# First stage of a two-block transformer kernel: output projection, norm, residual and router with tokens on partitions

## The chip, the cores and the metric

One core of one Trainium2 chip runs the whole program. The metric is device time in microseconds (us). The kernel before took 1844.75, 1839.3 and 1840.13 us in three timed runs; the median is 1840.13.

TensorE (PE) multiplies: a product takes 128-row weights (the stationary operand) and streams columns of the moving operand into PSUM, where up to 512 float32 columns of 128 partitions fill one bank. VectorE (DVE) and ScalarE (ACT) work on rows along the partitions, GpSimd (POOL) is a further engine, and SyncE (SP) issues most of the loads. Everything is float32; a float32 product appears in the trace as two instructions.

## The reference, cut to what matters

The model has a first block (attention with low-rank latents, a Fourier mixer, a mixture of 32 experts) and a second block of two layers. The input is 256 tokens of 1024 features. The change is between the attention of the first block and its experts:

```python
mix_x = jnp.concatenate([att_x, four_x], axis=-1) @ w_out[l]
x = x + g1 * rms_norm(mix_x, norm_attn_post[l])
hx2 = modulate(x, norm_ffn_pre[l], sh2, sc2)        # rms_norm(x, g) * (1 + sc2) + sh2
logits = h @ w_router + b_router                     # h = hx2
top_logit, top_idx = lax.top_k(logits, 4)
gates = jax.nn.softmax(top_logit, axis=-1)
# tokens of each expert in a block of their own, then per block:
g = jnp.minimum(xb @ w_gate[e] + b_gate[e], 7.0)
u = jnp.clip(xb @ w_up[e] + b_up[e], -7.0, 7.0)
y = (g * jax.nn.sigmoid(1.702 * g) * (u + 1)) @ w_down[e] + b_down[e]
```

The vectors g1, sh2, sc2 and g2 are four of the six rows of `silu(c) @ w_mod + b_mod`.

## The kernel before, in words

The program is a list of instructions for each engine, in a fixed order, with semaphores between them. An engine runs its own list in order, so that a wait holds everything behind it on that engine. The stages are `stage_first` (up to the router's tables), `stage_experts`, and `stage_second` for the second block.

**What lies on the partitions.** In `stage_first` features lie on partitions: `xT` and `mixT` are `[128, 8, 256]`, feature block times token. x is turned into `xT` at the very start (`turned(x, 4)`, L437, copies at L797 and L991). The output projection (`outward`, L649 to L658) makes 8 output blocks of 128 features by 8 input blocks: 64 products of 256 columns, in four PSUM banks (`BANKS`). The norm over features is then a sum over partitions: ScalarE squares each bank's copy (L943), a product with ones adds over partitions (L703), a 128x256 root and reciprocal follow (L947, L1162), the gain per feature is a scale per partition (L936), and VectorE multiplies and adds into `xT` (L1167, L1170). For the second norm the squares are collected by VectorE (L1159). The logits are four partial sums on 4 x 32 partitions (L713), added by a product with `quad` (L735), and h2 is `g2x` turned back into PSUM (L720), scaled per token and shifted (L1205).

**Routing.** VectorE takes the top eight of the logits (L1185), their indices (L1188), builds the 0/1 `mask` of the four picks (L1197, L1200), and the gates. TensorE counts, for each token and expert, the tokens ahead of it, by the strict triangle `stri` (L742), and the tokens of each expert (L745). VectorE makes `key` of it (rank of a picked token, -1 otherwise, L1229 and L1232), and the number of 64-token blocks of each expert, `more`, by four dependent comparisons (L1222 to L1225). TensorE turns key and gate (L756, L757), adds up `more` to the first block of each expert (L749 to L751), and spreads key and gates over 48 possible passes by `pick` (L768 to L770). The engines read the integer `table` for the loops.

**The experts.** `stage_experts` runs one pass for each block of 64 tokens (33 here: 32 experts and one with two blocks). A pass gathers the tokens by a product with the 0/1 matrix `sel` (L1370), turns them (L1376), adds biases (L1383), multiplies by gate and up weights (L1402) and down weights (L1455), and combines. The weights of one expert are 12.6 MB, in six parts. `ring` has ten places of 2 MB; `load_ahead` (L217) fills all ten from `stage_first`, each as soon as what it holds is no longer used. In the stage SyncE issues a part when a place is freed (L1334), which first happens after the first half of the gate products of pass 0.

**The order around the change.** SyncE's list has: w_mod blocks (2 MB each, L386, into three places in turn), w_out, one expert part after the last modulation sum, the expert biases, three and one parts after attention (`pv_ps`), one after `sh_ps`, three after the last projection product (`mix_ps` 4), and the last, where mix and h2's operands lay, after h2 (`h2_ok` 2). VectorE sums w_mod with `modulate_all` (L1025), in pieces between its attention steps. `keep_busy` (L133) issues filling products of 256 columns on TensorE.

Of the kernel before, what the change touches and what calls it, by code (L numbers as in the profile page):

```python
# [37 lines left out]
PAD = 16  # L38

# [23 lines left out]
for _name, _n in (("ident", P), ("ones", P), ("tri", QT * SEQ), ("iota", P), ("causal", QT * SEQ), ("cmpvalid", QT), ("etri", EXPERTS), ("gate16", 16), ("pad", 6),  # L63
                  ("twin", HD), ("heads16", 8), ("swap", P), ("ccos", P), ("csin", P), ("stri", QT * SEQ),
                  ("cos", SEQ), ("sin", SEQ), ("ncos", QT * SEQ), ("nsin", QT * SEQ), ("quad", EXPERTS), ("pad_last", 32)):
    CONST[_name] = (_at, _n)
    _at += _n
# [4 lines left out]
def shape_constants():  # L72
# [24 lines left out]
    strict = (n[:, None] < n[None, :]).astype(np.float32).reshape(QT, P, SEQ).transpose(1, 0, 2)  # L97
    put("tri", incl)
    put("stri", strict)
# [28 lines left out]
    put("quad", (np.arange(P)[:, None] % EXPERTS == e[None, :]).astype(np.float32))  # L128
# [91 lines left out]
def stage_first(nc, m, t):  # L220
# [6 lines left out]
    m.table = m.moe.sb("table", [1, PASSES + 1 + 2 * EXPERTS], I32)  # L227
# [12 lines left out]
    wr = s.sb("wr", [P, C, EXPERTS])  # L240
    br = s.sb("br", [1, EXPERTS])
# [8 lines left out]
    def early_tile(*shape):  # L250
# [4 lines left out]
        if len(shape) == 2:  # L255
# [28 lines left out]
    cosr, sinr, rb_q, rb_m = (m.spare[:, SEQ * j:SEQ * (j + 1)] for j in range(4))  # L284
# [10 lines left out]
    mixT, g2x = hT, hT  # L295
    mrow = zone[:, D:2 * D].rearrange("p (b n) -> p b n", b=2)
    acc1 = zone[:, 2 * D - 512:2 * D]
    idle = stats[:, 20:21]
    MOD_SLOT = (0, 4, 8, 0, 4, 8, 16, 8)
# [12 lines left out]
    rows_t, cols_ready, ssum, stds, rstds, normed, x_ps, copied_a, copied_v, silu_ready, silu_zero, mods_ps, mods_sb, moda_ps = (  # L312
        m.sem(n) for n in ("rows_t", "cols_ready", "ssum", "stds", "rstds", "normed", "x_ps", "copied_a", "copied_v", "silu_ready",
# [9 lines left out]
    msum_ps, msum_sb, modc_ps, modc_raw, modc_ok, crow_ps, sh_ps, sh_ok, mix_ps, mix_sb, mix_sq, mix_g, x1_mul, x1_ok, g2x_ok, x1_sq, x1_acc, lg_ps, part_ok, h2_ps, h2_ok = (  # L323
        m.sem(n) for n in ("msum_ps", "msum_sb", "modc_ps", "modc_raw", "modc_ok", "crow_ps", "sh_ps", "sh_ok", "mix_ps", "mix_sb", "mix_sq", "mix_g", "x1_mul",
                           "x1_ok", "g2x_ok", "x1_sq", "x1_acc", "lg_ps", "part_ok", "h2_ps", "h2_ok"))
# [3 lines left out]
    def scratch(shape, parts=P):  # L329
# [7 lines left out]
        if len(shape) == 2:  # L337
# [3 lines left out]
    part = scratch((SEQ,))  # L341
# [6 lines left out]
    key = scratch((QT, EXPERTS))  # L348
# [3 lines left out]
    tmp = scratch((3, PASSES), EXPERTS)  # L352
# [3 lines left out]
    logit_sb, top8, top_i, top_f, picked, peak, exped, g_chain, rank_ps, key_ok, more_chain, more_ps, table_ok, turned_ps, turned_sb, spread_ps, spread_sb = (  # L356
        m.sem(n) for n in ("logit_sb", "top8", "top_i", "top_f", "picked", "peak", "exped", "g_chain", "rank_ps", "key_ok", "more_chain",
                           "more_ps", "table_ok", "turned_ps", "turned_sb", "spread_ps", "spread_sb"))

    with nc.Block() as block:  # L360

        @block.gpsimd
        def _(pool):
# [4 lines left out]
            pool.memset(acc, 0.0).then_inc(zeroed, 1)  # L368

        @block.sync  # L370
        def _(sp):
# [49 lines left out]
            sp.wait_ge(sh_ps, 2)  # L421
            load_ahead(sp, m, t, 0, (3,))
# [7 lines left out]
        def _(pe):  # L430
# [10 lines left out]
            pe.wait_ge(x_in, 16)  # L441
            turned(x, 4)
# [23 lines left out]
            pe.wait_ge(copied_a, 2)  # L466
            pe.wait_ge(copied_v, 2)
# [183 lines left out]
            def outward(ks, cs, first=False, last=False):  # L651

                for k in ks:
# [2412 lines left out]
```

## Time and profile before

| what | us |
|---|---|
| timed runs | 1844.75, 1839.3, 1840.13 |
| median | 1840.13 |
| profiled execution | 1844.5 |
| its span | 1842.6 |
| TensorE busy | 1798.7 (98%) |
| VectorE busy | 601.2 (33%) |
| ScalarE busy | 372.7 (20%) |
| GpSimd busy | 10.9 (1%) |
| HBM read | 552.43 MB, 303 GB/s over the span |

Times in the rows are counted from the start of the span. A row of the timeline is a run of like instructions: start, length of the run, engine, line, operation, operands, and in brackets how long the engine had been idle and what ended that. Engine utilisation is no measure of need here: filling products count as busy.

### The profile page before, as it was taken

To read this page: it belongs to the slowest core of one execution; us is meant where nothing else is said; L and a number is where in the kernel's file an instruction comes from. 1 tells how busy PE (TensorE), PEld (TensorE's weight loads), DVE (VectorE), ACT (ScalarE), POOL (GpSimd) and SP (SyncE) were. 2 spreads that over 40 slices of the span, in tenths; PEclk is the share of its full clock that TensorE was granted. 3 is DMA by queue.
4 is the path that set the end of the run, shared out by engine and by line. 5 is a ranking of instruction groups with operands and counts; after the bars stand their busy time and mean duration, and the time that the engine had idled before them with its cause. 6 is when DMAs were issued, how large, how long until landed. Compare 5 with 4: busy or idle time off the path is not lost. (4 is left out here: it accounts for less than half of the span.)

```text
span 1842.6 us, 23153 instructions
## 1 busy us (share of the span) xinstructions
PE 1798.7 (98%) x9221; PEld 979.9 (53%) x9222; DVE 601.2 (33%) x1260; ACT 372.7 (20%) x725; POOL 10.9 (1%) x14
## 2 busy tenths in 40 slices
PE   7999999999999999999999999999999999999998
PEld 6757533333333333333333335767995466699843
DVE  1854410111111011111111113544655544345555
ACT  3221411111111111111111113332220033222101
POOL 0000000000000000000000000000000000000001
PEclk9999899999999999999999999999999999999999
DMA  9996599999999999999999999532446543124452
GB/s 370 393 188 270 237 412 430 431 430 431 433 431 432 430 431 432 431 431 431 432 432 431 431 430 358 174 140 92 151 149 241 160 183 137 46 92 147 151 175 99
DMA packets 104495, 558.61 MB, mean 303 GB/s; under 512 B 17128, under 2 KB 33997, under 8 KB 78701
## 3 DMA queue, kind: packets, MB, share of 16 engines
q1 hardware_dynamic: 101876, 553.06, 74.4%
q10 hardware_dynamic: 2554, 4.63, 1.8%
q8 instruction: 47, 0.77, 0.2%
q14 instruction: 18, 0.15, 0.0%
HBM read 552.43 MB, written 5.23 MB: 303 GB/s over the span
## 5 line engine op out<-in xcount | busy, mean ns | idle before, releaser
L1402 PE MATMUL ps<-ring,xs 128*64 128x512 f32 x2112 | 467.0, 593 | 10.9 <-DMA ring<-in_w_up 5.5
L1402 PEld LDWEIGHTS ps<-ring,xs 128*64 128x64 f32 x2112 | 150.7, 137 | 315.8 <-issue 291.6
L1455 PE MATMUL ps<-ring,actT 128*64 128x512 f32 x1056 | 233.9, 595 | 0.0
L2279 PE MATMUL ps<-ring 128*128 128x512 f32 x448 | 192.8, 592 | 0.0
L1528 DVE TENSOR_SCALAR hT<-ps 128x512 f32<-128x512 f32 x33 | 22.8, 692 | 449.7 <-PE ps L1402 449.7
L1455 PEld LDWEIGHTS ps<-ring,actT 128*64 128x64 f32 x1056 | 72.9, 137 | 158.7 <-issue 136.8
L2279 PEld LDWEIGHTS ps<-ring 128*128 128x128 f32 x448 | 84.9, 190 | 105.7 <-issue 105.7
L2014 PE MATMUL ps<-hT,ring 128*128 128x256 f32 x512 | 117.9, 383 | 3.5 <-ACT hT L1653 2.1
L1530 DVE TENSOR_SCALAR hT<-ps 128x512 f32<-128x512 f32 x33 | 22.8, 692 | 267.3 <-PE ps L1402 267.3
L2014 PEld LDWEIGHTS ps<-hT,ring 128*128 128x128 f32 x512 | 94.7, 190 | 22.2 <-issue 5.4
L2233 PE MATMUL ps<-hT,ring 128*128 128x128 f32 x768 | 93.4, 275 | 0.2 <-ACT hT L1653 0.2
L2233 PEld LDWEIGHTS ps<-hT,ring 128*128 128x128 f32 x768 | 89.5, 192 | 0.4 <-ACT hT L1653 0.3
L1506 ACT COPY y<-ps 128x512 f32<-128x512 f32 x33 | 19.3, 586 | 246.5 <-PE ps L1455 246.5
L1413 PE MATMUL ps<-y,selT 64*128 64x512 f32 x272 | 67.6, 615 | 0.7 <-ACT y L1506 0.7
L1499 ACT COPY xs<-ps 128x512 f32<-128x512 f32 x33 | 19.4, 587 | 236.2 <-PE ps L1376 236.2
L1370 PE MATMUL ps<-x_sb,sel 128*64 128x512 f32 x272 | 65.9, 606 | 0.3 <-PEq L360 0.3
L2233 PE MATMUL ps<-sq,ring 128*128 128x128 f32 x512 | 62.1, 275 | 0.0
L2233 PE MATMUL ps<-spare,ring 128*128 128x128 f32 x512 | 62.1, 275 | 0.0
L1495 ACT ACTIVATE hT<-hT 128x512 f32<-128x512 f32 x33 | 20.8, 630 | 193.7 <-DVE hT L1528 193.7
L2233 PEld LDWEIGHTS ps<-sq,ring 128*128 128x128 f32 x512 | 59.6, 192 | 0.0
L2233 PEld LDWEIGHTS ps<-spare,ring 128*128 128x128 f32 x512 | 59.6, 192 | 0.0
L2197 PE MATMUL ps<-x_sb,ring 128*128 128x256 f32 x256 | 57.4, 381 | 0.9 <-ACT x_sb L1636 0.9
(457 smaller groups left out, 1792.0 us busy)
## 6 DMA issues: line engine op xcount, KB each, us to landing
ring<-in_w_gate SPq DMA_DIRECT2D x64, 2048.0 KB, 29.0
ring<-in_w_down SPq DMA_DIRECT2D x64, 2048.0 KB, 29.1
ring<-in_w_up SPq DMA_DIRECT2D x64, 2048.0 KB, 27.3
ring<-in_mlp_w SPq DMA_DIRECT2D x16, 2048.0 KB, 8.7
ring<-in_mlp_w SPq DMA_DIRECT2D x32, 1024.0 KB, 5.4
ring<-in_w_mod SPq DMA_DIRECT2D x8, 2048.0 KB, 11.8
ring<-in_odd_w_in SPq DMA_DIRECT2D x6, 2048.0 KB, 10.1
ring<-in_w_mod SPq DMA_DIRECT2D x16, 512.0 KB, 11.0
```

What stands on the lines that cost most here:

```text
L1370: mm = pe.matmul(ps[SLOTS * half:SLOTS * (half + 1), TURN, :], sel[:, i, :], h2[:, i, half * 512:(half + 1) * 512], start=(i == 0), stop=( ...
L1402: mm = pe.matmul(ps[SLOTS * half:SLOTS * (half + 1), bank, :], xs[:, c % 4, c // 4 * SLOTS:(c // 4 + 1) * SLOTS], weights(v, 8 * part + c) ...
L1413: mm = pe.matmul(ps[:, COMB + 2 * i + half, :], selT[rows, i, :], y[rows, :], start=False, stop=stop, skip_group_check=True)
L1455: mm = pe.matmul(ps[SLOTS * half:SLOTS * (half + 1), Y, :], actT[:, f % 4, f // 4 * SLOTS:(f // 4 + 1) * SLOTS], weights(v, 16 + f)[:, hal ...
L1495: act.activation(sig, g, ACT.Sigmoid, scale=ALPHA).then_inc(sig_ok, 1)
L1499: act.copy(xs[:].rearrange("p b n -> p (b n)"), ps[:, TURN, :]).then_inc(xs_sb, 1)
L1528: v.tensor_scalar(g, ps[:, G, :], LIMIT, None, ALU.min).then_inc(g_ok, 1)
L1530: v.tensor_scalar(u, ps[:, U, :], -LIMIT, LIMIT, ALU.max, ALU.min).then_inc(u_ok, 1)
L2014: mm = pe.matmul(ps[:, bank, 0:SEQ], w[:, c, at:at + P], hT[:, c, :], start=(c == 0), stop=(c == C - 1))
L2197: mm = pe.matmul(ps[:, turn.banks[k], (d % 2) * SEQ:(d % 2 + 1) * SEQ], w[c // 4][:, c % 4, d * P:(d + 1) * P], mixT[:, c, :], start=(firs ...
L2233: mm = pe.matmul(out[:, i, :], weight[:, k, i * P:(i + 1) * P], token[:, k, :], start=(opens and k == 0 and i == 0), stop=(k == 3), skip_g ...
L2279: return pe.matmul(product_bank(layer, n), token, weight, start=(c == 0), stop=(c == PAIRS - 1))
```

## The change

It does the following, all in float32.

1. The output projection puts tokens on partitions: for token half `i` and feature half, 8 products of 512 columns each, 32 in all. Token half 0 is finished first, and its norm, residual, turning and logits are put between the products of half 1.
2. g1, 1 + sc2 (times their norm gains) and sh2 are spread to all partitions as rows by one-partition products (`rows_of`), and lie in `grow`, `scrow` and `shrow`. The gains come by four loads of a 512-row repeated on 32 partitions, which SyncE issues ahead of w_mod block 5, behind a wait for the rotary part.
3. The sums of squares are ScalarE's `accum_out` along the row; the root and reciprocal are 128x1. The residual is one fused multiply and add per 512 columns on x, which is loaded a second time. x is not turned at the start; `xT` is made from x1 afterwards.
4. The router's weights are multiplied by the scale column once (`wrm`), and the logits are 8 products per half from `xT`. h2 is a multiplication on GpSimd and a fused multiply and add on VectorE.
5. The rank is a product `mask.T @ rank`, experts on partitions, where `rank` is the strict triangle with 512 (`MARK`) on the diagonal. A picked token has its rank plus 512; `base` takes 512 off, so that others are negative. The number of blocks is one comparison with 4 limits and a sum.
6. The biases of pass 0 are put at the end of `stage_first`, and TensorE's `passes` load ahead of `turn_x`.
7. One expert part (`0, 3`) is issued after `msum_ps` instead of `sh_ps`.

```diff
-    put("stri", strict)
+    ranking = (n[:, None] < n[None, :]).astype(np.float32) + MARK * np.eye(SEQ)
+    put("rank", ranking.reshape(QT, P, SEQ).transpose(1, 0, 2))
...
+                if c == 5:
+                    sp.wait_ge(rope_done, 4)
+                    for j, name in enumerate(("norm_attn_post", "norm_attn_post", "norm_ffn_pre", "norm_ffn_pre")):
+                        src = t[name]
+                        sp.dma_start(gainrow[32 * j:32 * (j + 1), :], bass.AP(src.tensor, 512 * (j % 2), [[0, 32], [1, 512]])).then_inc(
+                            gainrow_in, 16)
                 second_part(c)
...
+            sp.wait_ge(pt_ps, HEADS)
+            sp.dma_start(x[:], stack(t["x"][0])).then_inc(x_in, 16)
+            sp.wait_ge(msum_ps, 1)
+            load_ahead(sp, m, t, 0, (3,))
             sp.wait_ge(pv_ps, HEADS)
...
-            pe.wait_ge(x_in, 16)
-            turned(x, 4)
+            keep_busy(m, pe, 4, 7)
...
                 for k in ks:
+                    i, half = k // 2, k % 2
                     for c in cs:
-                        for d in (2 * k, 2 * k + 1):
-                            mm = pe.matmul(ps[:, BANKS[k], (d % 2) * SEQ:(d % 2 + 1) * SEQ], w_out[:, c, d * P:(d + 1) * P], mixT[:, c, :],
+                        mm = pe.matmul(ps[:, BANKS[k], :], mixT[:, c, i * P:(i + 1) * P], w_out[:, c, 512 * half:512 * (half + 1)],
...
+            pe.wait_ge(pv_sb, 6)
+            rows_of(0, 0, 4)
+            outward((0, 1), (4, 5), last=True)
             pe.wait_ge(modc_raw, 2)
+            rows_of(0, 2, 2)
+            pe.wait_ge(row_a, 1)
+            pe.wait_ge(row_v, 1)
+            rows_of(1, 0, 4)
+            outward((2,), (6, 7, 0, 1), first=True)
...
+            outward((2,), (2, 3, 4, 5), last=True)
+            turned_back(0)
+            outward((3,), (6, 7, 0, 1), first=True)
+            logits(0, {0: 1, 4: 2})
+            outward((3,), (2, 3, 4, 5), last=True)
+
+            keep_busy(m, pe, 7, 4)
+            turned_back(1)
+            logits(1, {0: 3, 4: 4, 6: 5})
+            rank = cst(m, "rank")
+            pe.wait_ge(picked, 4)
+            pe.matmul(ps[0:EXPERTS, 5, 0:1], mask[:, 0, :], ones[:, 0:1], start=True, stop=False)
+            pe.matmul(ps[0:EXPERTS, 4, 0:SEQ], mask[:, 0, :], rank[:, 0:SEQ], start=True, stop=False)
+            keep_busy(m, pe, 7, 2)
+            pe.wait_ge(picked, 8)
...
+            row(1, 4, grow)
+            mix_power(0)
+            row(2, 2, scrow)
+            row(3, 4, shrow)
             act.wait_ge(crow_ps, 1)
+            act.copy(crow[:], ps[:, 3, 0:EXPERTS]).then_inc(crow_ok, 1)
+            x1_power(0)
+            mix_power(1)
+            x1_power(1)
...
+            row(1, 5, grow)
+            v.wait_ge(row_a, 1)
+            v.wait_ge(row_v, 1)
+            gained(0)
+            row(2, 3, scrow)
+            row(3, 5, shrow)
+            v.wait_ge(x_in, 32)
+            residual(0)
+            back(0, 0, 0, 4)
+            back(0, 1, 0, 4)
+            variance(0)
+            deviation(0)
+            v.wait_ge(row_a, 3)
+            v.wait_ge(row_v, 3)
+            scaled(0)
+            v.wait_ge(crow_ok, 1)
+            route(0)
+            gained(1)
+            residual(1)
+            back(1, 0, 0, 4)
+            variance(1)
+            back(1, 1, 0, 2)
+            back(1, 1, 2, 2)
+            deviation(1)
+            route(1)
...
+            for i in range(QT):
+                for half in range(2):
+                    k, cols = 2 * i + half, slice(512 * half, 512 * (half + 1))
+                    pool.wait_ge(x1_ok, k + 1)
+                    pool.tensor_tensor(mix[:, k, :], x[:, i, cols], scrow[:, cols], ALU.mult).then_inc(h2_mul, 1)
...
             gather()
-            biases(((0, G), (1, U)))
+            n = passes(pe)
+            pe.wait_ge(bdown_in, 32)
             pe.wait_ge(xrow_sb, 1)
             turn_x()
             keep_busy(m, pe, Y, 1)
-            n = passes(pe)
-            pe.wait_ge(bdown_in, 32)
```

The list with `mix_power` is ScalarE's, the one with `gained` VectorE's, the loop of `pool` GpSimd's. The helpers: `mix_power(i)` squares the two banks of half i and takes the root, `x1_power(i)` the same for x1; `gained` multiplies PSUM by `grow`; `residual` is x + mix * r; `turned_back(i)` and `back` make `xT` of half i; `route(i)` runs from the logits' fused multiply and add to the mask of half i; `scaled(i)` finishes h2 of half i, the last one after the tables.

## Rows read from the trace of the kernel before

**Rows 1.** Windows: stretch, length, busy PE PEld DVE ACT POOL, PEclk, DMA share, GB/s.
```profile
200.00:201.00 1.00, 0.77 (x6) 0.36 (x7) 0.27 (x1) 0.80 (x3) 0.00 (x0) 1.00 1.03 442
203.00:204.00 1.00, 1.00 (x5) 0.91 (x6) 0.46 (x3) 0.98 (x2) 0.00 (x0) 0.50 0.99 426
226.00:230.00 4.00, 4.00 (x20) 1.45 (x22) 0.00 (x0) 2.00 (x3) 0.00 (x0) 1.00 0.01 2
400.00:1120.00 720.00, 710.34 (x3412) 250.11 (x3408) 100.68 (x237) 121.00 (x183) 0.00 (x0) 1.00 1.01 431
```

**Rows 2.** Waits of TensorE, 225 to 1130 us: total, times, longest.
```profile
PE ps L1402 <- DMA ring<-in_w_up: 5.5, 6, 1.0
```

**Rows 3.** Timeline of TensorE: start, length, line, operands, number of instructions.
```profile
165.12 10.53 PE L656 MATMUL ps<-hT,ring 128*128 128x256 f32 x48
180.66 1.87 PE L694 MATMUL ps<-wr,modc 128*128 128x32 f32 x16
...
186.34 2.94 PE L703 MATMUL ps<-ring,consts_sb 128*128 128x256 f32 x12
...
218.61 3.68 PE L1370 MATMUL ps<-x_sb,sel 128*64 128x512 f32 x8 [0.30 <-PEq L360]
222.22 1.29 PE L1383 MATMUL ps<-brows,now 32*64 32x512 f32 x8
...
225.91 7.09 PE L1402 MATMUL ps<-ring,xs 128*64 128x512 f32 x32 [1.28 <-issue]
```

**Rows 4.** Timeline of SyncE: the issues of expert parts.
```profile
186.54 0.33 SPq L217 DMA_DIRECT2D ring<-in_w_gate  x1
...
208.75 0.33 SPq L217 DMA_DIRECT2D ring<-in_w_down  x1
229.60 3.76 SPq L1334 DMA_DIRECT2D ring<-in_w_down  x2
```

**Rows 5.** Timeline of VectorE: picks, h2, gate steps, last copy.
```profile
205.28 1.06 DVE L1200 SCALAR_TENSOR_TENSOR zone<-consts_sb,zone 128x32 f32<-128x32 f32 x6
206.26 2.47 DVE L1205 SCALAR_TENSOR_TENSOR x_sb<-ps,stats,ring 128x1024 f32<-128x1024 f32 x2
208.64 0.21 DVE L1209 TENSOR_TENSOR zone<-zone 128x64 f32<-128x64 f32 x1
208.89 0.22 DVE L1211 TENSOR_REDUCE zone<-zone 128x2 f32<-128x64 f32 x1
...
217.47 0.25 DVE L1255 COPY gates<-ps 128x96 f32<-128x96 f32 x1
```

**Rows 6.** Timeline of ScalarE: a Square, and a sum read out.
```profile
184.74 0.63 ACT L943 ACTIVATE ring<-ring 128x512 f32<-128x512 f32 x1
...
1831.58 0.19 ACT L2609 ACTIVATION_READ_ACCUMULATOR sq<-x_sb 128x1 f32 x1
```

**Rows 7.** Around w_mod block 5: two windows, and VectorE's timeline.
```profile
84.00:92.00 8.00, 8.00 (x31) 5.52 (x30) 7.83 (x12) 1.49 (x2) 0.00 (x0) 1.00 1.02 425
...
87.76 0.42 DVE L1071 TENSOR_TENSOR ring<-ring,x_sb 128x256 f32<-128x256 f32 x1
...
110.00:120.00 10.00, 8.17 (x33) 5.16 (x32) 6.38 (x12) 3.75 (x10) 0.00 (x0) 1.00 0.91 102
...
120.84 4.86 DVE L1025 SCALAR_TENSOR_TENSOR ring<-ring,silu 128x1024 f32<-128x1024 f32 x4
```

**Rows 8.** Timeline of TensorE: the same 16 transposes early and later.
```profile
12.98 3.65 PE L437 MATMUL ps<-consts_sb,ring 128*128 128x128 f32 x16 [2.31 <-DVE cols L988]
...
51.23 1.91 PE L437 MATMUL ps<-consts_sb,zone 128*128 128x128 f32 x16
```

**Rows 9.** Timeline near the end: GpSimd and VectorE side by side.
```profile
1827.68 0.68 DVE L2983 TENSOR_TENSOR x_sb<-x_sb,ring 128x512 f32<-128x512 f32 x1
...
1831.17 1.27 POOL L1887 TENSOR_TENSOR ring<-x_sb,ring 128x512 f32<-128x512 f32 x1 [540.69 <-DVE x_sb L2875]
1831.70 1.28 DVE L2993 TENSOR_TENSOR x_sb<-x_sb,ring 128x512 f32<-128x512 f32 x1
```

More of the change, by code:

```diff
@@ L38 @@
 PAD = 16
+MARK = 2.0 * SEQ
 HD = 64
@@ L696, in _ @@
-            pe.wait_ge(pv_sb, 6)
-            outward((0, 1, 2, 3), (5,), last=True)
-            pe.wait_ge(sh_ok, 2)
-            for k in range(4):
-                pe.wait_ge(mix_sq, k + 1)
-                for half in range(2):
-                    mm = pe.matmul(ps[:, 3, 0:SEQ], ones, sq[:, k % 2, half * SEQ:(half + 1) * SEQ],
-                                   start=(k == 0 and half == 0), stop=(k == 3 and half == 1))
-                mm.then_inc(var_ps, 1)
-            keep_busy(m, pe, 2, 9)
@@ new lines, in _ @@
+            mm.then_inc(turned_ps, 1)
+            pe.wait_ge(pick_chain, 5)
+            for i in range(QT):
+                pe.matmul(ps[:, 2, i * PASSES:(i + 1) * PASSES], keyT[:, i, :], pick, start=(i == 0), stop=False, skip_group_check=True)
+            pe.wait_ge(pick_chain, 7)
+            for i in range(QT):
+                mm = pe.matmul(ps[:, 2, i * PASSES:(i + 1) * PASSES], ones[0:EXPERTS, :], base[:], start=False, stop=True, skip_group_check=True)
+            mm.then_inc(keys_ps, 1)
@@ L753, in _ @@
-            pe.wait_ge(key_ok, 1)
-            pe.wait_ge(g_chain, 5)
-            for i in range(QT):
-                pe.transpose(ps[0:EXPERTS, 4, i * P:(i + 1) * P], key[:, i, :], ident)
-                mm = pe.transpose(ps[0:EXPERTS, 4, (2 + i) * P:(3 + i) * P], gate[:, i, :], ident)
-            mm.then_inc(turned_ps, 1)
-            pe.wait_ge(more_chain, 9)
-            pe.matmul(ps[0:1, 3, 0:PASSES], more[:, 3:4], pick, start=True, stop=True).then_inc(more_ps, 1)
-            pe.wait_ge(h2_ok, QT)
@@ L771, in _ @@
-            mm.then_inc(spread_ps, 1)
+            pe.wait_ge(m.brows_in, 32)
+            pe.wait_ge(now_sb, 2)
+            for half in range(2):
+                for b in range(2):
+                    mm = pe.matmul(ps[SLOTS * half:SLOTS * (half + 1), b, :], m.now[EXPERTS * b:EXPERTS * (b + 1), :],
+                                   m.brows[EXPERTS * b:EXPERTS * (b + 1), 512 * half:512 * (half + 1)], start=True, stop=False,
+                                   skip_group_check=True)
+            mm.then_inc(m.bias_ps, 1)
@@ new lines, in residual @@
+            def residual(i):
+                v.wait_ge(row_std, 2 * i + 1)
+                v.reciprocal(mix_r[:, i:i + 1], mix_r[:, i:i + 1]).then_inc(row_inv, 1)
+                v.wait_ge(row_inv, 2 * i + 1)
+                v.wait_ge(mix_g, 2 * i + 2)
+                for half in range(2):
+                    k, cols = 2 * i + half, slice(512 * half, 512 * (half + 1))
+                    v.scalar_tensor_tensor(x[:, i, cols], mix[:, k, :], mix_r[:, i:i + 1], x[:, i, cols], ALU.mult, ALU.add).then_inc(x1_ok, 1)
@@ new lines, in deviation, with scaled @@
+            def deviation(i):
+                v.wait_ge(row_std, 2 * i + 2)
+                v.reciprocal(x1_r[:, i:i + 1], x1_r[:, i:i + 1]).then_inc(row_inv, 1)
+                v.wait_ge(row_inv, 2 * i + 2)
+            def scaled(i):
+                v.wait_ge(h2_mul, 2 * i + 2)
+                for half in range(2):
+                    k, cols = 2 * i + half, slice(512 * half, 512 * (half + 1))
+                    ins = v.scalar_tensor_tensor(h2[:, i, cols], mix[:, k, :], x1_r[:, i:i + 1], shrow[:, cols], ALU.mult, ALU.add)
+                ins.then_inc(h2_ok, 1)
@@ L1242, in _ @@
-            v.scalar_tensor_tensor(base[:], tmp[:, 0, :], float(-SLOTS), pick, ALU.mult, ALU.mult).then_inc(more_chain, 1)
-            v.tensor_copy(m.pick[EXPERTS:2 * EXPERTS, :], pick)
-            for half in range(2):
-                v.tensor_copy(m.now[EXPERTS * half:EXPERTS * (half + 1), :], pick[:, 0:1].to_broadcast([EXPERTS, SLOTS]))
-            v.wait_ge(more_ps, 2)
-            v.tensor_copy(m.table[:, 0:PASSES + 1 + EXPERTS], ps[0:1, 3, 0:PASSES + 1 + EXPERTS])
-            v.tensor_scalar(m.table[:, PASSES + 1 + EXPERTS:], ps[0:1, 3, PASSES + 1:PASSES + 1 + EXPERTS], -1.0, None, ALU.add).then_inc(table_ok, 1)
```

396 lines of the change are left out of this document (180 added, 216 removed).

## The prediction, made before the changed kernel ran

> **What bounds the kernel now.** I read the page first: TensorE is busy 98% of the span, so only what it waits for, or what runs on it slowly, can be won. The windows then split the span. From the first expert pass to about 1120 us the DMA engines move 431 GB/s at a share of 1.01 and TensorE is busy 710 of 720 us [rows 1]; its largest waits there are six short ones for up weights, 5.5 us in all, with gate weights some 10 [rows 2]. So this stage is a conveyor. It is started by two things: the first expert matmul at 225.91 us, and the first ring slot that it frees, which lets SyncE issue again at 229.60 [rows 3, 4]. Between the landing of what is issued at 208.75 and that issue DMA comes to have nothing to do (share 0.01 from 226 to 230) [rows 1]. Whatever moves 225.91 and 229.60 moves everything behind them, one for one. The change works in the 60 us ahead of that point, so I price only this: when does L1402 begin?
>
> The TensorE timeline says what fills those 60 us. The output projection is over when L703 begins at 186.34 (48 instructions of L656 in 10.53: 0.44 per 256-column product, two instructions each) [rows 3]. From there to 225.91 TensorE mostly fills time, and ScalarE and VectorE hand work to each other: Square and gain per block, reciprocal of a 128x256 tile, two passes over 128x512 per block, squares collected, logits, the picks of both halves to 206.34, h2 (2.47 for two), then key, block counts and tables to 217.72 [rows 5, 6]. The granted clock is 0.50, 1.2 GHz, at 203, and the gather at 218.61 is still at half rate [rows 1, 3].
>
> **The change part by part.** Clock times are those of the profiled execution.
>
> *Projection turned round.* 64 products of 256 columns become 32 of 512: 2 x 0.44 = 0.88 at the old rate; I take 0.86. The products left at 165.1, where the modulation columns are transposed, are 20 x 0.86 = 17.2. Ahead of the last one TensorE now has more to do: six products that copy a row (g1, scale, shift) to all partitions, the router's constant row (2.1, as now), eight transposes of x1 (1.0, half of the 16 at 51.23) and eight logit products of token half 0 (1.9, the price of L694, x16 in 1.87) [rows 3, 8]. A one-partition 512-column product is not in the trace: between 0.32 (L1383, x8 in 1.29, four products on 32 partitions) and 0.88 (L656, doubled). I take 0.86, since columns, not partitions, set L656; six are 5.2. Sum 17.2 + 5.2 + 2.1 + 1.0 + 1.9 = 27.4, so the last product ends at 192.5 instead of 186.3: **6.2 us later**. Half 0 is done meanwhile: its mix is complete at 170.3, VectorE has x1 at 176.5, ScalarE its squares at 181.3 (they stand behind the copy of the constant row at 179.5), h2 at 186.7. None of this delays TensorE or the second half; ScalarE is free for the latter's first square at 185.
>
> *From the last product to the last pick.* Now 186.3 to 206.34: 20.0 us. After, with ScalarE's and VectorE's durations for 128x512: handover 0.2; Square with its sum read out 0.63 + 0.19; gain product 0.69 (square root 0.3 and reciprocal beside it); two residual passes 1.4 to the second; turning 0.6; three copies and the deviation 1.1; the last logit products 1.1; handovers between them 0.8; then one half's routing. That chain is one fused multiply-add, top-8, index, cast, four picks, at about 0.25 per dependent small instruction (L1209 at 208.64, L1211 at 208.89) with 0.35 for the index pair: 2.1 [rows 5, 6]. Sum 8.8, last pick at 201.3: **11.2 saved on this leg**. The price is in the handovers: 0.04 to 0.2 each, a dozen of them, so 1 us less to 2.5 us more.
>
> *From the last pick to the first gather.* Now 206.34 to 218.61: 12.3. h2's 2.47 of VectorE stood first; in its place only half 1 is left (1.3), and later. The marked rank matrix gives ranks already with experts on partitions: no key on VectorE, no key transposes, and a count by one comparison and one sum instead of four dependent steps. After: two gate steps 0.5, wait for the count 0.3, comparison and sum 0.5, reciprocal and scaling 0.65, wait for the block starts 0.25, four steps to pick and base 0.9, table 0.4, h2 1.3, keys, selection and gates 0.95, and 0.9 from VectorE's end to the gather as now (217.72 to 218.61): 6.7 [rows 3, 5]. **5.6 saved.** The biases of pass 0 (1.29 at full clock, 8 instructions) now stand on TensorE at the end of this leg, beside VectorE's last copies; at half clock they take 2.2 and put the gather at 208.6 instead of 208.0. I cost them at nothing, 0.6 if the clock is low.
>
> *Gather to first expert matmul.* Now 7.3. Without the biases the turn of xrow waits only for ScalarE's copy, and one register load goes ahead: **0.5 saved** (0 to 1.3, from the 1.28 that L1402 waited) [rows 3]. Total 11.2 + 5.6 + 0.5 - 6.2 = **11.1 us**; L1402 begins at 214.8.
>
> *DMA.* Blocks 0, 2 and 9 of the ring wait for the last projection product: issued at 192.7 instead of 186.54, 6.3 MB at 431 GB/s, with 2 us of latency, land by 209.4; the gate block, which L1402 needs, lands by 200. The last, behind h2 (206.0), lands by 214.3 and is not used until the down product, 20 us into pass 0 [rows 4]. The first freed slot is at 214.8 + 3.65 = 218.5, so nothing is owed to the conveyor; margin 4.2 us. That is also the cap: past 15 us of gain the conveyor starts no earlier. x (1 MB) comes in again behind one ring block, by 165, and is wanted at 174.7.
>
> *Ring block ahead of the attention.* SyncE now waits for the rotary part (L1071, 88.18) and issues four gain rows before w_mod block 5, which until now it issues without this wait, so it goes out at 90. VectorE wants it at 120.84. At three quarters of the 425 GB/s moved from 84 to 92, blocks 5 and 6 land by 104 [rows 7]. Nothing is late.
>
> *The start.* 16 transposes of x and four copies go; seven filling products come. TensorE's order at 12.98 is held by normalised x, not by these. Value 0; gain up to 1.7 if the transposes at 12.98 run as those at 51.23 (3.65 against 1.91) [rows 8]; loss none, since seven products at half rate, 0.88 each, from about 4 on end at 10.1, and 12.98 waits for none of them.
>
> *GpSimd.* It gets four multiplications of 128x512, 1.27 each. They end three us or more before h2 needs them, but run beside VectorE. I take 0, since the instructions that follow x1 on VectorE read PSUM; at most 0.6 twice, for at 1831.70 a VectorE product of two SBUF operands beside such a multiplication took 1.28 instead of 0.68 [rows 9]. The Trainium skill (SBUF — State Buffer, Who interferes with whom) says that a VectorE instruction with two SBUF inputs and a GpSimd one that reads SBUF exclude each other for a whole instruction; the row agrees, and it speaks against this edit if the residual pass of the next block comes second.
>
> The profiled execution took 1844.5 (span 1842.6); the median of the three runs is 1840.13. I take the difference of 11.1 to the median: **1829 us**. Its own range is a gain of 6 to 15.
>
> **The rivals.**
> *The clock stays low.* TensorE is now idle in pieces between 194 and 201, as it was from 194 to 202, after which 0.50 was granted [rows 1]. If that holds from about 198 until past the first expert matmuls, the small products on the leg double (+1), the biases end late (+0.6) and the first eight products of L1402, 1.8 us now, run at half rate (+1.8), with handovers near their long end (+2): gain 6, 1834. For it: the fall before under almost the same pattern. Against: filling products stand in both gaps.
> *Clock up early.* The filling products from 4 on raise the clock before 12.98 and it holds over the gap there: 1.7 more, 1827; with the gather at full rate too (half of 3.68), 3.5 more, 1825.5. The rows speak half against it: between 201 and 203 the clock fell although TensorE had been busy 0.77 of 200 to 201 and more after it. The Trainium skill (TensorE: Matmul & The Clock Gate, What's actually happening) has the clock half rate by default, released by activity and lost again by idleness; by that alone it would stay up over a gap as short as the one before 12.98. The fall at 202, with hardly an idle moment, does not agree.
> *No overlap.* The last half's leg is no shorter because the in-order engines hold it behind half 0: then only the 5.6 and the 0.5 stand against the 6.2, 1840. Against it: ScalarE is done with half 0 seven us before the last product.
> *Slower: w_mod block 5 is late.* Issued at 90 with block 6, it shares the engines with the 4 MB of the bias table; from 110 to 120 these move only 102 GB/s at a share of 0.91 [rows 7]. 4.46 MB at that rate end at 133.7, 12.9 us after VectorE wants it, and attention moves with it: 12.9 - 11.1 = 1.8 slower, 1842; it decides from a landing at 120.84 on. Against it: from 84 to 92, with the table under way, 425 GB/s were moved.
>
> **How the numbers follow.** Forecast 0.55; clock low 0.17; clock early 0.15; no overlap 0.08; block late 0.05. Eight in ten: 1824 (clock up everywhere, at the cap) to 1836 (clock low, with half of GpSimd's price and long handovers; and the three runs themselves spread by 5). 0.3% is 5.5 us, about what this kernel's measurement can tell: faster needs under 1834.6. Forecast and early clock count as faster but for 0.03; low clock for two thirds; no overlap is the same; block late is half same, half slower, and 0.02 for what I have not seen: faster 0.80, same 0.15, slower 0.05.
>
> **What would show it.** L1402 begins near 215 and SyncE's next issue comes near 218.5; the last projection product ends near 192.5; the last pick near 201; h2 of half 0 before 188; the shift is the same at 1120 us. Wrong: VectorE waiting for w_mod after 120, a start of L1402 later than 220, waits for weights in the expert stage above 10 us, or a last product after 194.

## The result: the changed kernel is a little slower, and its profile

| | us | runs |
|---|---|---|
| kernel before, median (range) | 1841.47 (1839.12 to 1844.75) | 18 |
| changed kernel, median (range) | 1844.57 (1842.38 to 1845.77) | 18 |
| ratio after to before, 95% interval | 1.0014 [1.0008, 1.0020] | |
| profiled execution, span | 1844.5, 1842.6 before; 1843.72, 1841.9 after | |

Forecast were 1829 us and a range of 1824 to 1836. The change costs 3 us (0.14%, inside what was called "the same"). The profiled execution of before lies 3 us above its median, that of after 1 us below, so the spans differ by -0.7 us where the medians differ by +3.1; no trace shows where these +3.1 arise. I compare places inside the two spans, and use the medians for totals. The experiments were timed in other sessions than the changed kernel, and the median of the kernel before lay between 1841.06 and 1843.61 in them. So a difference to the changed kernel is safer by the ratios, which were taken beside the kernel before, and known to about 2 us only.

The first view is SyncE's timeline of the changed kernel. The four gain rows keep SyncE from 87.54 to 102.82; only then does it issue w_mod block 5. Its next expert part behind the first freed slot goes out at 228.18, against 229.60 [rows 4] and a forecast of 218.5.
```profile
68.38 0.95 SPq L406 DMA_DIRECT2D ring<-in_w_mod  x2
87.54 5.28 SPq L434 DMA_DIRECT2D early_consts<-in_norm_attn_post  x2
92.86 9.92 SPq L434 DMA_DIRECT2D early_consts<-in_norm_ffn_pre  x2
102.82 29.01 SPq L406 DMA_DIRECT2D ring<-in_w_mod  x3
...
209.26 0.33 SPq L217 DMA_DIRECT2D ring<-in_w_down  x1
228.18 3.76 SPq L1383 DMA_DIRECT2D ring<-in_w_down  x2
```
The windows of the same kernel (stretch, length, busy time of the engines, PEclk, DMA share, GB/s) answer to [rows 7]: where before moved 425 GB/s, after moves 102, at a share of 0.92. In this window the packets are those of the 4 MB store of the bias table (the queue of ScalarE); what moved 425 GB/s before were w_mod blocks 5 and 6, issued at 72.80 and 84.19. TensorE then stands idle for four microseconds and goes on at half clock.
```profile
84.00:92.00 8.00, 8.00 (x32) 5.78 (x31) 7.90 (x11) 1.49 (x2) 0.00 (x0) 1.00 0.92 102
...
128.00:132.00 4.00, 0.00 (x0) 0.00 (x0) 4.00 (x5) 0.00 (x0) 0.00 (x0) 0.70 0.45 193
132.00:136.00 4.00, 3.77 (x9) 3.09 (x10) 2.67 (x5) 0.00 (x0) 0.00 (x0) 0.50 0.88 303
```
VectorE's timeline says who waited: it wants block 5 at 120.2 and gets it at 126.61 (in brackets: idle before, and for what).
```profile
126.61 4.87 DVE L1056 SCALAR_TENSOR_TENSOR ring<-ring,silu 128x1024 f32<-128x1024 f32 x4 [6.41 <-DMA ring<-in_w_mod]
```
TensorE's timeline of the changed kernel, from the projection to the first expert matmul, answers to [rows 3]. The modulation sum (L725) begins at 164.55, 7.4 us after its counterpart in the kernel before; everything behind it carries that shift. To be seen: the row products (L690) are cheap, the last projection product (L681) ends at 197.3, the gather is 5.1 us earlier than before, and then 4.70 us go to a wait for b_down.
```profile
164.55 1.92 PE L725 MATMUL ps<-ring,consts_sb 128*32 128x512 f32 x16
...
172.63 1.13 PE L690 MATMUL ps<-zone,consts_sb 1*128 1x512 f32 x4
...
177.32 1.14 PE L690 MATMUL ps<-zone,consts_sb 1*128 1x512 f32 x8
...
193.61 3.68 PE L681 MATMUL ps<-ring,hT 128*128 128x512 f32 x8
...
210.69 1.99 PE L801 MATMUL ps<-brows,now 32*64 32x512 f32 x8
...
213.51 3.68 PE L1419 MATMUL ps<-x_sb,sel 128*64 128x512 f32 x8 [0.32 <-PEq L373]
221.89 1.13 PE L1425 MATMUL ps<-consts_sb,xrow 128*128 128x128 f32 x4 [4.70 <-DMA y<-in_b_down]
...
223.89 7.68 PE L1451 MATMUL ps<-ring,xs 128*64 128x512 f32 x32
```
On VectorE the last picks begin at 204.53 and end at 205.35 (one microsecond before [rows 5], in spite of the 7.4):
```profile
204.53 0.82 DVE L1242 SCALAR_TENSOR_TENSOR zone<-consts_sb,zone 128x32 f32<-128x32 f32 x3
```
In the expert stage TensorE's waits for weights fell (up weights 4.7 us in all against 5.5 [rows 2]), but a steady pass, from one gather to the next, takes 27.08 us instead of 26.99. From the first freed slot to the transposes that open stage two the changed kernel needs 908.7 us (228.18 to 1136.91), before 907.7. After them both need 705.0 to 705.3.

So the distance to the forecast has three places: block 5 late, b_down late, a longer pass. Theory A: the four small loads ahead of block 5 cost about 8 us and the change is sound behind them. Theory E: b_down costs 3 to 5. Theory C: the order of two waits on ScalarE makes the pass longer.

### The profile page after: what moved, and what is told of

The parts are those of the page before. It is cut to its first block and busy times, and to the rows that moved or that the text cites. A ratio compares the mean times of both kernels' runs of the same rounds, so it can differ in the third digit from the quotient of the medians.

```text
span 1841.9 us, 22968 instructions
## 1 busy us (share of the span) xinstructions
PE 1792.6 (97%) x9121; PEld 961.1 (52%) x9122; DVE 598.7 (33%) x1262; ACT 366.9 (20%) x719; POOL 16.7 (1%) x18
## 5 line engine op out<-in xcount | busy, mean ns | idle before, releaser
L1451 PE MATMUL ps<-ring,xs 128*64 128x512 f32 x2112 | 467.2, 593 | 7.9 <-DMA ring<-in_w_up 4.7
L1451 PEld LDWEIGHTS ps<-ring,xs 128*64 128x64 f32 x2112 | 150.8, 137 | 313.1 <-issue 293.1
```

The lines of the kernel that those rows point to most:

```text
L1451: mm = pe.matmul(ps[SLOTS * half:SLOTS * (half + 1), bank, :], xs[:, c % 4, c // 4 * SLOTS:(c // 4 + 1) * SLOTS], weights(v, 8 * part + c) ...
```

## The experiments

### The gain rows (theory A)

a1_gains_behind moves the rotary wait and the four loads behind blocks 5 and 6; a2_wait_alone leaves the wait and moves only the loads; d1_two_loads leaves the wait and two loads ahead of block 5.
```diff
 for c in range(3, C):
+    if c == 7:
+        sp.wait_ge(rope_done, 4)        # a1: wait and loads here
+        ... four loads of gainrow ...
     sp.wait_ge(modb_done, 6 if c == 7 else c - 2)
     if c == 6:
         sp.wait_ge(proj_ps, 6)
-    if c == 5:
-        sp.wait_ge(rope_done, 4)
-        ... four loads of gainrow ...
     second_part(c)
```


> The changed kernel, with the four gain-row loads and their wait for the rotary part moved behind w_mod blocks 5 and 6 (ahead of block 7's wait). Theory A (block 5 comes late because of what now stands ahead of it on SyncE): VectorE's 6.4 us wait for w_mod goes, the modulation sum at 164.55 comes back to about 157, and the first expert matmul comes up to 7 us earlier; the time falls by 4 to 7 us against the changed kernel, to about 1838 to 1840, unless the queue of expert parts takes some of it back. Rival B (a new wait later on swallows it, since the ring loads are then the bound): the modulation sum is at 157, but the first freed slot is less than 2 us earlier and the time stays within 2 us of 1844.6.

Measured 1836.19 us, ratio to before 0.9968 [0.9956, 0.9981]: 8.4 us under the changed kernel by the medians, 8.5 (give or take 2.6) by the ratios. SyncE's timeline, and a window of DMA as it was before:
```profile
68.20 15.30 SPq L406 DMA_DIRECT2D ring<-in_w_mod  x4
87.61 0.79 SPq L431 DMA_DIRECT2D early_consts<-in_norm_attn_post  x2
88.44 0.89 SPq L431 DMA_DIRECT2D early_consts<-in_norm_ffn_pre  x2
```
```profile
84.00:92.00 8.00, 8.00 (x32) 5.75 (x31) 7.90 (x11) 1.49 (x2) 0.00 (x0) 1.00 1.02 432
```
The same loads at the same 87.6 us cost SyncE 1.7 us when blocks 5 and 6 are in flight, 15.2 when nothing but the store is. The store runs in both cases (from 84 to 92 us it moved 0.82 MB in the changed kernel and 0.41 MB here), so it is not the store alone that holds SyncE; no run moved or shortened it, and why issues take so long stays open.

> The changed kernel, with the wait for the rotary part left ahead of w_mod block 5 and only the four loads moved behind block 6. Theory A1 (the wait does the harm, since it issues block 5 at 87 instead of 73): block 5 still lands late and VectorE waits 3 us or more for it at 120. Rival A2 (the four small loads do it, they held SyncE from 87.5 to 102.8): block 5 is issued at 88, block 6 behind it, and VectorE does not wait at all.

Measured 1836.20 us, 0.9972 [0.9960, 0.9984]. The wait by itself harms nothing: VectorE has no wait for w_mod. Block 5 goes out behind it, at 87.97, and its landing (23.5 us after its issue, at 111.5) is in time. Block 6, issued next, needs 29.1 us. The small loads are as slow to issue behind it. Timeline of SyncE, then block 5's issue with its KB and time to landing:
```profile
67.77 25.56 SPq L406 DMA_DIRECT2D ring<-in_w_mod  x4
93.38 9.94 SPq L430 DMA_DIRECT2D early_consts<-in_norm_attn_post  x2
103.36 2.04 SPq L430 DMA_DIRECT2D early_consts<-in_norm_ffn_pre  x2
...
ring<-in_w_mod SPq DMA_DIRECT2D x1, 2048.0 KB, 23.5
```


> The changed kernel with only two of the four small loads (those of the norm after attention) ahead of block 5 of w_mod, still behind the wait for the rotary positions; the other two stand behind block 6. Theory H (each pair of small loads holds SyncE, 5.3 us and 9.9 us in the changed kernel, and any load issued after 87.5 us, while the 4 MB store of the bias matrix has the 16 DMA engines to itself, needs 20 to 26 us to land whatever its size): block 5 is issued at 92.5 to 93.5, lands at 116 to 119, ahead of VectorE's want of it at 120.2; no wait for w_mod, w_up of expert 0 back at 156 instead of 163, the first freed ring slot at 220 to 221, and 1836 to 1837. Rival J (the small packets of the four loads slow the transfers beside them, so any of them ahead of block 5 makes it late): a wait of 3 us or more for w_mod remains, 1839 to 1842. Rival K (the hold is of fixed length, about 15 us, whatever the number of loads): block 5 is issued at 102 to 103 and lands at 126, 1844.

Measured 1835.81 us, 0.9970 [0.9958, 0.9981]: theory H, at the very edge. With two loads ahead, block 5 goes out at 93.78 and lands 27.0 us later, at 120.8 (I had said 119 at most); VectorE's instruction that needs it begins at 121.03 without a wait. The first freed slot came at 219.5.
```profile
88.46 5.28 SPq L429 DMA_DIRECT2D early_consts<-in_norm_attn_post  x2
93.78 9.96 SPq L406 DMA_DIRECT2D ring<-in_w_mod  x2
103.79 9.20 SPq L429 DMA_DIRECT2D early_consts<-in_norm_ffn_pre  x2
```
```profile
121.03 4.86 DVE L1061 SCALAR_TENSOR_TENSOR ring<-ring,silu 128x1024 f32<-128x1024 f32 x4
```
The third and fourth issue take SyncE 9.9 us together whatever they load, 64 KB or 2 MB. So two loads ahead cost nothing, with 0.2 us to spare, and four cost 8 us; three were not run.

### The b_down wait (theory E)

```diff
-            pe.wait_ge(bdown_in, 32)      # ahead of turn_x()
...
             act.copy(xs[:]..., ps[:, TURN, :]).then_inc(xs_sb, 1)
+            act.wait_ge(bdown_in, 32)     # ahead of clearing the rest of y
```


> The changed kernel, with one wait moved from TensorE to ScalarE: TensorE no longer waits for the b_down rows before it turns the first gathered rows; ScalarE waits for them after its copy of those rows and before it clears the rest of y, which is where they are first needed. All else, the late block 5 of w_mod too, stays. Theory E (in the changed kernel the b_down rows, whose loads stand behind the expert ring's loads, end the first pass's start, 4.7 us of wait in its trace): the first expert-weight products begin 4 to 5.5 us earlier than 223.9, the first freed ring slot is at 223 to 225 instead of 228.2, and if the ring's next loads had slack the time is 3 to 4.5 us lower, 1840 to 1841.5. Rival F (DMA-bound from there on: the waits for expert weights in the second stage's end or in the first passes take it back): the first freed slot comes earlier, TensorE's waits for weights grow by as much, the time stays within 1 us of 1844.6. Rival G (the half clock of that stretch, not the wait, has the price): the wait goes, the weight products before the first freed slot lengthen from 7.7 to 9 us or more, and 1 to 3 us are won.

Measured 1840.12 us, 0.9992 [0.9983, 1.0001]: 4.4 us under the changed kernel by the medians, 4.1 (give or take 2) by the ratios, theory E. TensorE's timeline:
```profile
216.85 0.75 PE L1425 MATMUL ps<-consts_sb,xrow 128*128 128x128 f32 x4 [0.68 <-ACT xrow L1529]
217.43 0.60 PE L136 MATMUL ps<-consts_sb 128*128 128x256 f32 x2
218.85 7.09 PE L1451 MATMUL ps<-ring,xs 128*64 128x512 f32 x32 [0.82 <-ACT xs L1531]
```
The wait is gone, the products begin 5.0 us earlier, and SyncE's issue comes at 222.54 instead of 228.18.

### The length of a pass (theory C)

```diff
                 act.copy(xs[:]..., ps[:, TURN, :]).then_inc(xs_sb, 1)
-                act.wait_ge(selt_ps, i + 1)
                 act.wait_ge(comb_ps, i + 1)
+                act.wait_ge(selt_ps, i + 1)
                 act.copy(selT[:]..., ps[:, G, 0:QT * P]).then_inc(selT_sb, 1)
```
a3_swap has this edit on the changed kernel, b1_before_swap on the kernel before.

> The changed kernel, with the two waits ahead of ScalarE's copy of selT in the expert loop written in the other order; nothing else. In the changed kernel a pass takes 27.08 us instead of 26.99, and all of it lies between the combining products and the start of that copy (0.19 instead of 0.10). Theory C (the cost is the step from the late wait, which stands in an instruction of its own, to the copy): with the late wait on the copy itself the pass is 26.99 or less and the time falls by 3 us, to 1841.5. Rival D (the cost is in where the instructions of the loop lie, not in the order of the waits): the pass stays at 27.08 and the time at 1844.6.

Measured 1842.18 us, 1.0002 [0.9993, 1.0011]: 2.4 us under the changed kernel by the medians, 2.2 (give or take 2) by the ratios, pass 26.98.

> The kernel before, with the same two waits in the other order. Theory C: the copy starts up to 0.05 us sooner, the pass is 26.94 to 26.99, and the time is 0 to 1.5 us below 1841.5. Rival D: nothing moves, or the pass takes 0.09 more and the time is 3 us longer.

Measured 1841.61 us, 0.9999 [0.9989, 1.0009]: nothing, pass 26.98 (26.99 before). The order alone does not explain a difference between two kernels that both have it. So I shifted the loop's code on ScalarE instead, with one and with three waits for a value long reached, ahead of the loop.
```diff
+            for _pad in range(1):         # p3_pad: range(3)
+                act.wait_ge(x_ps, 1)
             act.wait_ge(xt_ps, 1)
             act.copy(xs[:]..., ps[:, TURN, :]).then_inc(xs_sb, 1)
```


> The changed kernel with one more wait on ScalarE, for a semaphore value that is there already, ahead of the expert stage's loop (before the copy of the first gathered rows); nothing in the loop changes. It shifts where the loop's instructions lie in ScalarE's instruction stream by one. If placement decides whether the step from the end of the combining products to the copy of selT takes 0.10 or 0.19 us: in one of this kernel and the one with three more waits the step is 0.10 again, the steady pass 26.98 to 26.99 and the time 2 to 3 us below the changed kernel's 1844.6. If the order of the waits decides (or another engine): 0.19 and 27.08 in both, the same time as the changed kernel within 1 us.

> As the kernel p1_pad, with three more waits instead of one. If placement decides: the step of the selT copy is 0.10 in at least one of the two, the steady pass 26.98 to 26.99 there, 1841.5 to 1842.5. If the order of the waits decides: 0.19 and 27.08 in both, 1844 to 1845.

Measured 1842.27 us (1.0003 [0.9993, 1.0012]) and 1842.43 us (1.0003 [0.9994, 1.0013]), pass 26.99 in both. The copy of selT in ScalarE's timeline, idle before it in brackets, of the changed kernel and of p1_pad:
```profile
324.62 0.37 ACT L1550 COPY selT<-ps 128x256 f32<-128x256 f32 x1 [1.71 <-PE ps L1462]
```
```profile
322.54 0.37 ACT L1552 COPY selT<-ps 128x256 f32<-128x256 f32 x1 [1.61 <-PE ps L1462]
```
The same loop behind one more wait has the step 0.10 us shorter. A wait outside the loop can act on it only by where the loop's instructions come to lie, as far as I can see; that is an argument, not a measurement. Theory C fell in its first form: swapping the waits was one more way to change the code. Why the changed kernel's placement is bad stays open.

What a longer pass costs is not 33 times 0.09. Five or six passes in the middle of the stage take 29.0 to 29.2 us in every kernel, with waits for up and gate weights: 12.6 MB at 431 GB/s are 29.2 us by estimate, so there the loads set the pace. From the first freed slot to the end of these passes it takes 552.5 to 554.3 us in all fourteen traces, whether a pass has 26.98 or 27.08. Behind them one wait of 0.9 to 1.0 us for weights is left, in the next pass, and only there does a longer pass add to the time: 353.4 to 353.6 us to stage two with the short pass, 354.8 to 354.9 with the long one. That is 1.3 us, from 12 passes. TensorE's timeline of a6_all (short pass) and a5_both (long), two kernels of the next section, at the two ends of this stretch:
```profile
771.87 1.89 PE L1419 MATMUL ps<-x_sb,sel 128*64 128x512 f32 x8
1125.33 1.91 PE L2088 MATMUL ps<-consts_sb,x_sb 128*128 128x128 f32 x16
```
```profile
768.73 1.89 PE L1419 MATMUL ps<-x_sb,sel 128*64 128x512 f32 x8
1123.51 1.91 PE L2088 MATMUL ps<-consts_sb,x_sb 128*128 128x128 f32 x16
```
The medians of a3_swap, p1_pad and p3_pad lie 2.1 to 2.4 us under the changed kernel's, by the ratios 2.0 to 2.2, give or take 2; what they have beyond 1.3 us is within that. The waits for weights are 9.9 us in a6_all and 7.9 in a5_both, so a part of what a shorter pass wins is paid back there.

### All together

a5_both is a1 with a4's edit, a6_all has a3's too.

> Two of the three edits of the kernel a6_all: the small loads and their wait behind block 6 of w_mod, and the b_down wait on ScalarE; ScalarE's waits ahead of the selT copy as in the changed kernel. If the costs add up: 1836.2 less 3.2 us (b_down wait) = 1833 to 1833.5 with a steady pass of 27.08; between a1_gains_behind's 1836.2 and a6_all's 1830.0. If the pass is 26.98 here too, as the one-wait and three-wait pads showed it can be by placement alone: 1830. If the b_down wait was worth nothing once block 5 is on time: 1836.

> Three edits on the changed kernel at once: the four small loads and the rope wait ahead of block 7's wait of w_mod instead of block 5's; the b_down wait on ScalarE as in the kernel a4_bdown; ScalarE's two waits ahead of the copy of selT in the other order. If the three costs are separate (theory): 1836.2 of the first edit alone, less 2.5 to 3 us for the shorter steady pass (26.98 instead of 27.08, 33 passes), less 2 to 3.2 us for the b_down wait (3.2 us in the trace with the first edit alone): 1830 to 1832, first freed ring slot at 218 to 219. If the expert ring's first loads bind (rival: the fifth slot group of expert 0 and what follows it land only about 210 to 212 and later, the DMA engines being full from the second stage's start): TensorE waits for weights in the first pass, the b_down part gives under 1 us, 1833 to 1834. If the pass length goes by the code's placement alone and not by the order of the waits: 27.08 again, 1833 to 1835.

| kernel | us | ratio [95%] |
|---|---|---|
| a5_both | 1830.26 | 0.9934 [0.9915, 0.9952] |
| a6_all | 1829.97 | 0.9932 [0.9919, 0.9946] |
| a5_again | 1830.62 | 0.9937 [0.9925, 0.9949] |
| a6_again | 1829.71 | 0.9929 [0.9917, 0.9942] |

a5_both was 3 us better than its sum, so both ran again. Beside a1's edit, a4's is worth 5.6 to 5.9 us (1836.19 to 1830.62 and 1830.26), more than the 3.2 us that TensorE waits for b_down in a1's trace.

> The kernel a5_both once more, beside a6_all's, in more rounds: its first four times lay 3 us below the sum of the separate costs, and its profiled execution had a steady pass of 27.08 us, 0.10 us above a6_all's. If the short pass is worth its 33 times 0.10 us here as it was in the changed kernel (a3_swap, p1_pad, p3_pad: 2.2 to 2.4 us): this kernel's median lies 2 to 3.5 us above that of a6_again, at 1832 to 1833.5. If the pass length no longer sets the time with the earlier start: both at 1830 to 1830.5, and the pass starts of both traces at 600 us would have to differ by less than the starts of the first pass do.

> The kernel a6_all once more, beside a5_both's. If the short pass has its worth: 1829.5 to 1830.5, with the steady pass at 26.98. If the first times were chance: both kernels at 1830 to 1832 within 1 us of each other.

The two are within 1 us: the expected 2 to 3.5 us did not come. The pass is worth 1.3 by the traces. They show a second thing that differs: TensorE's clock. These are windows of a5_again, then of a6_again.
```profile
194.00:198.00 4.00, 3.31 (x21) 1.92 (x20) 2.56 (x15) 1.39 (x5) 0.45 (x1) 1.00 1.03 432
198.00:202.00 4.00, 3.66 (x34) 3.24 (x38) 3.67 (x17) 1.93 (x7) 0.00 (x0) 0.83 0.99 426
202.00:206.00 4.00, 3.70 (x14) 1.25 (x16) 0.00 (x0) 0.00 (x0) 0.00 (x0) 0.50 1.01 434
206.00:210.00 4.00, 3.14 (x12) 1.05 (x8) 1.02 (x5) 1.16 (x2) 0.00 (x0) 0.82 1.02 416
```
```profile
194.00:198.00 4.00, 4.00 (x16) 2.40 (x15) 2.36 (x12) 1.23 (x4) 0.32 (x1) 0.55 1.01 424
198.00:202.00 4.00, 3.92 (x24) 2.41 (x24) 2.92 (x14) 1.86 (x7) 0.00 (x0) 0.50 1.00 430
202.00:206.00 4.00, 4.00 (x21) 2.71 (x20) 1.28 (x5) 0.11 (x1) 0.00 (x0) 0.50 1.01 430
206.00:210.00 4.00, 3.70 (x14) 1.36 (x10) 0.00 (x0) 0.00 (x0) 0.00 (x0) 0.50 1.00 430
```
In a5_again the clock falls to 1.2 GHz at about 201 and is back at 2.4 GHz from about 207; in a6_again it falls at about 194 and is back from about 211. The instructions there are the same, and those between the fall and the return run at half rate. The first freed slot comes at 214.32 in a5_again and 217.25 in a6_again, and in the first pair of profiles at 214.75 (a5_both) and 217.60 (a6_all). So a5 is ahead by 3 us at the start, loses 1.3 of it in the passes, and its profiled spans are 1.8 to 1.9 us shorter; the medians do not show this. Whether the order of the waits or only chance put the fall there stays open. a6_all beats both kernels of this case, by 0.7% against before (11 to 14 us, the two times it ran).

## Why the prediction was wrong, step by step

**The step that failed** is "Ring block ahead of the attention ... Nothing is late". Two of its numbers were wrong. It let block 5 go out at 90, so it gave the four gain rows 1.8 us of SyncE behind the wait; they took 15.3 (87.54 to 102.82). And it took the rate of 84 to 92 us in [rows 7], 425 GB/s, as one that a later block 5 would get, though this was the rate of blocks 5 and 6 themselves: with them out of that window, 102 GB/s were moved, all of it the store's, and the block needed 23.7 us from issue to landing, where the forecast had 14 for blocks 5 and 6 together. Either error alone would have done no harm: by estimate, 102.82 + 14 is 117 and 90 + 23.7 is 114, both ahead of 120.2, and in a2_wait_alone the block, issued at 87.97, did land in time, at 111.5. Together they give 126.5. The rival "w_mod block 5 is late" had the place and the sign right, and the time from which a landing counts as late (120.84 [rows 7]; it landed about 126.6). It had 0.05 of the chance. Its own estimate, a landing 12.9 us late, was long, since it gave the loads the 102 GB/s that were the store's: the landing was 6.4 late, plus a fall of the clock behind it. In all 7.4 at L725, 8.4 us in a1_gains_behind.

**A step left out**: b_down. The prediction had the turn of xrow wait "only for ScalarE's copy". The diff moves TensorE's wait for b_down from behind that turn to ahead of it (L1451 stands behind the wait either way), and ScalarE issues those two loads only when the gather begins: at 213.44, against 218.57 before. Before, the last ring block had been issued at 208.75 [rows 4] and was through: the DMA view from 205 to 226 us has
```profile
ring<-in_w_down SPq DMA_DIRECT2D x1, 2048.0 KB, 8.6
y<-in_b_down ACTq DMA_DIRECT2D x2, 64.0 KB, 1.9
```
and the changed kernel's from 209 to 226
```profile
ring<-in_w_down SPq DMA_DIRECT2D x1, 2048.0 KB, 13.2
y<-in_b_down ACTq DMA_DIRECT2D x2, 64.0 KB, 7.2
```
The change shortens the way from the last projection product, which frees the ring blocks, to the gather. So b_down now meets the ring's load in flight. It lands at about 221 us in both kernels, but here everything else is ready earlier. The prediction traced what the ring blocks would be late for, and not what would be late for them. 4.4 us by a4_bdown, 5.6 to 5.9 where block 5 is on time.

**A step that nobody priced**: the pass. The expert loop's code was costed at nothing since no instruction of it changes its work; by the traces it cost 1.3 us. No view of the kernel before could tell this.

**The row products** were mis-sized on the safe side: six at 0.86 made 5.2 us; they took 1.13 + 1.14 = 2.27. One of their twelve instructions takes 0.59 to 0.69 us, so that they can fit into 2.27 only by running beside each other; the rows of `ones` that they use lie at partitions 0, 32, 64 and 96. So the bound of 0.32 was nearly met for another reason than a cheap product. With 0.7 us won at the start (at 87.03 instead of 87.76 by L1102, once L1071 [rows 7]; the 16 transposes of [rows 8] took 3.16 instead of 3.65), the last projection product ends at 189.04 where block 5 is on time (a6_all), not 192.5; in the changed kernel at 197.3, for the 7.4.

**Last product to last pick**, forecast 8.8: 8.1 in the changed kernel (197.3 to 205.35), 8.7 in a6_all. Right, so the overlap of the first half works, and "no overlap" is refuted.

**Last pick to gather**, forecast 6.7: 8.2 in the changed kernel, 9.9 in a6_all. Too short, and the clock is why. TensorE's tail of this leg in the two kernels is the same instructions at half rate (the biases 1.99 where [rows 3] had 1.29; I had allowed 0.6 for it, for one of them). The rival "the clock stays low" named this, but looked for the fall at 198; it was at about 208 in the changed kernel and at 194 in a6_all. The prediction also had the fall at 202 in the kernel before come "with hardly an idle moment"; TensorE was busy 2.91 of 194 to 198 and 2.95 of 198 to 202.

**GpSimd.** Its first multiplication of half 1 starts at 199.68, inside VectorE's second residual step (199.51 to 200.25), a step that reads two SBUF operands and runs after the first half of x1 is released, where the prediction had only steps that read PSUM. VectorE's step took 0.74, as without GpSimd (0.75); GpSimd's took 1.72 instead of 1.27. In [rows 9] GpSimd had started first, and VectorE paid. So the price was real, and fell on the engine that nobody waited for.

**Gather to L1451**, forecast 6.8: 6.3 in a6_all, 10.4 in the changed kernel, for b_down.

**The sum.** In a6_all L1451 begins at 213.91 (forecast 214.8) and the first slot is free at 217.6 (218.5):
```profile
213.91 7.09 PE L1451 MATMUL ps<-ring,xs 128*64 128x512 f32 x32 [0.77 <-ACT xs L1531]
```
Its 1829.97 us is within a microsecond of the 1829 forecast, but that is another kernel, with three further edits, and the nearness is in part luck: 3.5 us too much up to the last product and 3.2 too little behind the picks cancel. The chances do not add up either: by the parts that it names, faster comes to 0.78, same to 0.19 and slower to 0.045, not 0.80, 0.15 and 0.05. The rule that a start moved by so much moves the end by as much also held: from the first freed slot to stage two 907.2 to 909.0 us, and 705 from there, in every kernel but a3_swap, p1_pad and p3_pad (906.0, 906.1, 907.0).

## What to carry to other kernels

A load that is small in bytes is not small to the queue that issues it: while a long store of short rows fills the DMA engines, put large, urgent loads ahead of small ones. Read a window's rate as belonging to what was in flight in it; take that transfer out and the rate is another. In a loop that has a stretch bound by its loads, time saved per pass ahead of that stretch is lost in it; count only the passes behind. Before costing a reordering at its compute, list every wait that the diff moves, with the transfer behind it and what that transfer stands behind.

## What the runs showed that was not expected

A 64 KB load issued into the store took 20.0 us to land, and one of 2 MB 23.7: so time to landing hardly depended on size there. This is DMA by queue from 96 to 110 us in the changed kernel (packets, MB, share of the engines), and the issues with KB and median time to landing:
```profile
q10 hardware_dynamic: 694, 1.42, 89.8%
q1 hardware_dynamic: 99, 0.14, 2.7%
...
ring<-in_w_mod SPq DMA_DIRECT2D x2, 2048.0 KB, 23.7
early_consts<-in_norm_ffn_pre SPq DMA_DIRECT2D x2, 64.0 KB, 21.4
```
The 694 packets of the store took 14 x 16 x 0.898 / 694 = 0.29 us each. The Trainium skill (DMA: Bandwidth & Descriptors, Queues, rings and completion order) has each DMA engine take turns between its queues packet by packet. By that, and if its 32 rows of 2 KB are spread evenly over 16 engines, such a load should by estimate be through in a few turns of 0.29 us once its packets stand at the engines. The loads took 20 us, so this rule alone does not give their time. Whether their packets stood at the engines or had not got there, no trace tells. In a2_wait_alone the queue of the loads moved 2 packets from 84 to 94 us, with two 2 MB blocks issued at 88, and the store's 520. Where block 5 was in flight already, the same loads landed in 6.5 to 7.2 us (a1_gains_behind).

TensorE's clock fell between 194 and 203 us in all variants with block 5 on time, though TensorE was busy 2.97 of 4 us or more in the windows ahead of each fall; where it falls moves by 6 us between a5_again and a6_again, which have the same instructions there, and the first freed slot by 3.
